# Row products, block sums and the order of the attention rounds in a chain of two small transformer blocks

## The chip, the cores and the metric

The kernel runs on one core of a Trainium2 chip. The metric is the device time of one execution in microseconds; the kernel before has a median of 1409.66 us in 3 runs (1409.54 to 1411.51). Everything is computed in float32.

## What is computed

Input x has 256 tokens of width 1024. It passes two blocks of two layers each.

Block 1, per layer: `mod = silu(c) @ w_ada + b_ada` is cut into shift, scale and gate; `u = rms_norm(x, g) * (1 + scale) + shift`; `z = u @ w_in` is cut into queries, keys, values and gates of three attentions (A: 8 heads over the 64 best keys of an indexer; B: window with sinks, 8 query heads and 2 key heads; C: stick-breaking, 8 heads) and three merge gates. Each attention's output times `silu(gate)` goes through its own matrix, the three are added under `sigmoid(m)`, and `x + gate * (merged @ w_out)` is the next x. A last `rms_norm` ends the block.

Block 2 has the 256 tokens of x and 256 context tokens. Per layer: `mod` as above, from a condition for x and one for the context (so two columns); `h = x * (1 + scale) + shift`; four mixers of 256 columns each: H (a gated linear scan in both directions), G (grouped attention), F (differential attention), N (window attention with sinks); queries of x see the keys of x and of the context. Then `x_new = layer_norm(alpha * x + gate * (y @ w_out))`. In layer 0 the context gets the same treatment; in layer 1 it only gives keys, values and the scan's final states. The kernel reads 222.6 MB from HBM, nearly all of it weights, each once.

## The kernel before

**Layout.** Activations lie transposed: channels on the 128 partitions, tokens (256) in the free dimension, 8 blocks of channels. Weights come in units of 1 MB (128 x 2048 numbers) through a ring of five slots; SP's queue starts the transfer of unit n + 5 when unit n has been used (`stream`). A unit of a projection is 16 matmuls of 128x128 by 256 columns, which the profile shows as 32 records. Results go to one of three PSUM banks ("events"), in turn; an item waits until the bank that it takes has been drained (`drained`) and signals when it is full (`full`).

**Order.** The whole program is one list of items per section (`prologue`, `one0`, `one1`, `two0`, `two1`). Every engine walks the same list and does its own part of each item, in order; semaphores count the parts. `one0` and `one1` are block 1's layers, and `one1` also has the context's attentions of block 2 at its end; `two0` and `two1` are block 2's layers. There is no planner: the lists are written by hand, and `weave`, `behind`, `lay` and `lay_scan` put items between one another.

**Attention.** A section has a list of jobs (10, 18, 16, 16). A job has these steps: logits (TensorE, to a PSUM tensor that all jobs share), mask or maximum (VectorE), exponentials (ScalarE), scaling (VectorE, item "soft"), transposition ("turn": TensorE, then a copy to PT by ScalarE), value product ("mix": TensorE, then a copy to y by VectorE). For the stick-breaking jobs (C) turn is a product with triangular matrices, then clamp (VectorE), exponential (ScalarE) and select (GpSimd). `weave` makes rounds of them; for round n the list is: logits n, slot 2n-1 of `fill`, soft n, mix n-2, turn n-1, slot 2n. The slots hold projections, the picks of the 64 best keys, scan steps and the like. `("half", item)` does the first half of a unit's work, so that its halves can stand in two slots.

**Modulation.** `mod` for later layers is computed in two ways. "By rows" (`mvr` and `mvs`, the two halves of a unit): the unit holds 256 columns of the matrix as rows, and VectorE multiplies a 128x1024 half with silu(c) on all partitions and sums it, one instruction per condition (line 1751); `bias` adds b_ada. "By TensorE" (`mva`, line 965): silu(c) is the 128x32 weight in four strips, the result is copied out (line 1739), transposed (`ada`, line 979), added up over the strips (lines 1778 and 1781). In the kernel before, block 2's layer-1 groups 0 to 3 (shift and scale) go by TensorE in `two0`, groups 4 and 5 (gate) in `two1`.

**Norms.** Squares of the 8 blocks of channels are added over blocks and partitions by 8 matmuls with a matrix of ones (`stats` line 1001; `mean` and `var` line 1330). Squares of block 1's x come from ScalarE after each `out` (line 1494); mean and variance of block 2's layer norm are taken from x after each `out`/`outb` (evictions at lines 2072 and 2084).

**Scan.** The mixer H is computed in nine levels. `prep` makes the operands of a level (GpSimd gaps at lines 2282 to 2288, ScalarE exponential, VectorE products at lines 2153 and 2155), `level` is 8 matmuls into two banks (line 1257) and VectorE copies them under a mask (line 2172), `hout` is the last product.

## Time and profile before

| what | value |
|---|---|
| median of 3 runs | 1409.66 us |
| profiled execution, its own time | 1411.23 us |
| its span, first to last instruction | 1409.5 us |
| TensorE busy | 1367.1 us, 97% |
| weight loads busy | 1123.4 us, 80% |
| VectorE busy | 655.1 us, 46% |
| ScalarE busy | 419.7 us, 30% |
| GpSimd busy | 165.5 us, 12% |
| moved by DMA | 224.93 MB, 160 GB/s over the span |
| mean granted clock of TensorE | 0.995 of full |

PE is TensorE's matmuls, PEld its weight loads, DVE VectorE, ACT ScalarE, POOL GpSimd, SP the queue that starts transfers. L1022 is line 1022 of the kernel. x32 is a count of records. A matmul's end is modelled, so that the times from one group's start to the next one's say more than the lengths. A group of rows of one line shows the start, the length, the engine, the line, the tiles and, in brackets, the engine's idle time before it and what ended it.

### The profile page before, as it was taken

How to read it: one execution, taken by the hardware profiler on the slowest of the kernel's cores; microseconds unless marked ns; L12 is line 12 of the kernel's file. 1: busy time of each engine (PE TensorE's matmuls, PEld its weight loads, DVE VectorE, ACT ScalarE, POOL GpSimd, SP SyncE). 2: the span in 40 equal slices, each digit the busy share in tenths (PEclk: the TensorE clock that was granted, in tenths of full speed). 3: DMA queues.
4: the chain of work that ended last, by engine and by line, in shares of the span. 5: the costliest groups of instructions: out<-in, count | busy, mean ns of one | idle time of the engine just before them, and what ended most of it. 6: DMA issues, size and time to landing. Idle time of an engine off the chain costs nothing.

```text
span 1409.5 us, 19281 instructions
## 1 busy us (share of the span) xinstructions
PE 1367.1 (97%) x7590; PEld 1123.4 (80%) x7590; DVE 655.1 (46%) x1457; ACT 419.7 (30%) x773; POOL 165.5 (12%) x191
## 2 busy tenths in 40 slices
PE   6999999999999999999999999999999999999996
PEld 4888787888888888888888888877777788887764
DVE  1447776445223554424144421245683632566466
ACT  2322222411021222333323313332343512433442
POOL 0201200000020120001021100003230000242000
PEclk9999999999999999999999999999999999999998
DMA  9636555568534433444333433455332343422240
GB/s 385 245 110 255 193 213 210 222 262 310 187 121 149 179 120 120 180 162 145 126 118 124 145 120 116 142 190 187 123 111 90 102 152 121 182 103 90 90 150 31
DMA packets 31916, 224.93 MB, mean 160 GB/s; under 512 B 3921, under 2 KB 4049, under 8 KB 5073
## 3 DMA queue, kind: packets, MB, share of 16 engines
q1 hardware_dynamic: 31824, 223.68, 43.0%
q8 instruction: 61, 1.00, 0.3%
q14 instruction: 31, 0.25, 0.0%
HBM read 222.62 MB, written 1.05 MB: 159 GB/s over the span
## 4 chain that ended last, share of the span: by engine, by line
PE 88%; DVE 7%; issue 2%; ACT 1%; DMA 1%; POOL 1%; SPq 0%; DVEq 0%; ACTq 0%; POOLq 0%
PE event L1022 45%; PE event L1013 9%; PE event L1166 6%; PE event L1230 5%; PE logits L1098 4%; PE mixed_out L1154 3%; PE turns L1117 3%; PE event L1257 2%; PE event L1191 2%; PE event L1196 2%; PE logits L989 1%; PE event L965 1%; PE event L1330 1%; PE event L1001 1%; DVE logits L1850 1%
## 5 line engine op out<-in xcount | busy, mean ns | idle before, releaser
L1022 PE MATMUL event<-u,ring 128*128 128x256 f32 x3072 | 683.3, 381 | 9.0 <-DMA ring<-in_w 4.3
L1022 PEld LDWEIGHTS event<-u,ring 128*128 128x128 f32 x3072 | 576.9, 190 | 101.5 <-issue 18.2
L1013 PE MATMUL event<-ring,u 128*128 128x256 f32 (+1 forms) x704 | 151.1, 372 | 0.0
L1013 PEld LDWEIGHTS event<-ring,u 128*128 128x128 f32 x704 | 127.4, 190 | 21.4 <-issue 5.3
L2308 POOL TENSOR_TENSOR raw<-raw,tables 128x512 f32<-128x512 f32 (+1 forms) x28 | 44.6, 1593 | 701.9 <-DVE turned L1824 518.8
L1427 ACT ACTIVATE region<-event 128x512 f32<-128x512 f32 x72 | 43.0, 597 | 275.4 <-PE event L1022 275.1
L1463 ACT ACTIVATE S<-logits,stat 128x512 f32<-128x512 f32 (+2 forms) x160 | 83.9, 536 | 130.0 <-DVE stat L1865 120.6
L1230 PE MATMUL event<-region,ring 128*128 128x256 f32 x384 | 85.0, 380 | 0.0
L1166 PE MATMUL event<-region,ring 128*128 128x256 f32 x384 | 84.2, 380 | 0.0
L1230 PEld LDWEIGHTS event<-region,ring 128*128 128x128 f32 x384 | 72.3, 190 | 12.2 <-issue 2.7
L1166 PEld LDWEIGHTS event<-region,ring 128*128 128x128 f32 x384 | 72.7, 190 | 10.8 <-issue 1.0
L1479 ACT ACTIVATE PT<-turns 128x1024 f32<-128x1024 f32 (+1 forms) x52 | 44.7, 860 | 81.7 <-PE turns L1117 81.2
L1842 DVE TENSOR_REDUCE stat<-logits 128x2 f32<-128x1024 f32 (+1 forms) x32 | 39.2, 1224 | 53.2 <-PE logits L1098 52.7
L1098 PE MATMUL logits<-region 64*128 64x256 f32 (+4 forms) x320 | 59.9, 475 | 2.9 <-ACT S L1463 1.4
L1751 DVE CUSTOM_DVE_ANT_0 region<-ring,u 128x1024 f32<-128x1024 f32 x48 | 59.1, 1231 | 1.7
L2172 DVE COPY_PREDICATED region<-tables,event 128x512 f32<-128x512 uint32 x42 | 30.9, 735 | 58.5 <-PE event L1257 57.4
L1924 DVE COPY region<-mixed_out 128x256 f32<-128x256 f32 (+3 forms) x60 | 21.7, 362 | 75.3 <-PE mixed_out L1154 65.1
L1154 PE MATMUL mixed_out<-PT,region 128*64 128x128 f32 (+2 forms) x584 | 54.8, 296 | 0.8 <-ACT PT L1479 0.8
L1154 PEld LDWEIGHTS mixed_out<-PT,region 128*64 128x64 f32 x584 | 38.3, 136 | 16.5 <-issue 13.4
L1117 PE MATMUL turns<-consts,S 128*128 128x128 f32 x336 | 47.9, 281 | 0.0
L1751 DVE CUSTOM_DVE_ANT_0 region<-ring,region 128x1024 f32<-128x1024 f32 x32 | 40.4, 1263 | 11.2 <-issue 5.0
L2282 POOL TENSOR_TENSOR region<-region 128x256 f32<-128x256 f32 x24 | 16.0, 667 | 248.6 <-PE event L1257 156.5
(246 smaller groups left out, 1343.7 us busy)
## 6 DMA issues: line engine op xcount, KB each, us to landing
ring<-in_w SPq DMA_DIRECT2D x196, 1024.0 KB, 4.9
region<-in_quick SPq DMA_DIRECT2D x8, 1024.0 KB, 18.7
region<-in_rows SPq DMA_DIRECT2D x1, 1536.0 KB, 8.3
tables<-in_two SPq DMA_DIRECT2D x1, 1472.0 KB, 7.9
x<-in_x SPq DMA_DIRECT2D x1, 1024.0 KB, 7.2
u<-in_cond_rows SPq DMA_DIRECT2D x1, 1024.0 KB, 7.7
x<-in_ctx SPq DMA_DIRECT2D x1, 1024.0 KB, 7.1
out<-x SPq DMA_DIRECT2D x4, 256.0 KB, 2.2
```

The lines of the kernel that those rows point to most:

```text
L1013: ins = mm(bank[:, t * 256:t * 256 + width], mem.u[:, q, k, t * P:(t + 1) * P], wt[:, k * 256:k * 256 + width], start=k == 0, stop=k == KB ...
L1022: ins = mm(bank[:, j * 256:(j + 1) * 256], wt[:, k * 256 + j * P:k * 256 + j * P + P], mem.u[:, q, k, :], start=k == 0, stop=k == KB - 1)
L1098: ins = mm(out, q, k, start=True, stop=True)
L1117: ins = eng.transpose(mem.TR[:, i * P:(i + 1) * P], S[:, at:at + P], c["ident"])
L1154: ins = mm(out, value_of(mem, job, m, kt), turned[:, :, kt, :], start=kt == 0, stop=kt == tiles - 1)
L1166: ins = mm(bank[:, j * 256:(j + 1) * 256], wt[:, at:at + P], mem.one["y"][:, 4 * br + k, :], start=k == 0, stop=k == 3)
L1230: ins = mm(bank[:, j * 256:(j + 1) * 256], wt[:, at:at + P], src[:, k, :], start=k == 0, stop=k == KB - 1)
L1427: act(dst, split2(bank), func, scale=scale).then_inc(drained[e % BANKS], 1)
L1463: ins = act(S[:, m * K:(m + 1) * K], mem.LG[:, m * K:(m + 1) * K], ACT.Exp, bias=stat[:, 1, m:m + 1], accum_out=stat[:, 2, m:m + 1])
L1479: act(mem.PT[:, n % 2, 0:cols], mem.TR[:, 0:cols], ACT.Copy).then_inc(sems["turns_copied"], 1)
L1751: ins = eng.tensor_tensor_reduce(out=mem.scratch, in0=part, in1=times, scale=1.0, scalar=0.0, op0=ALU.mult, op1=ALU.add, accum_out=mem.mod ...
L2308: tt(shape(mem.raw), shape(mem.raw), wide(cosine, width // T), ALU.mult).then_inc(mine, 1)
```

## The change

It does the following:

- In `weave` the order of round n becomes: logits n, the scan levels of slot 2n-1, mix n-2, then `hout` and the rest of slot 2n-1, soft n, turn n-1, slot 2n. Levels in slots behind a turn stay where they were.
- `lay_scan` puts the latent scans' steps in every second slot, which is one that follows logits, so one step a round; before, a step came every 1.4 (`two0`) or 1.34 slots (`two1`).
- Block 2's layer-1 groups 0 to 3 (8 units) are computed by rows: two units at the end of `one0`'s list of them, six in `one1`. The units of `mva` and the `ada` steps of `two0` are gone.
- A unit by rows with two conditions stands whole (four instructions) behind a job's turn; before, its halves stood behind logits and turn. Units with one condition stand whole behind the logits of jobs that are not C. Behind the merges and projections at the end of `one0` the halves stay single.
- In `one1` the first feed of the context (`mod`, `feed`) moves from logits 4 to logits 7, the context's first projections come after five of the six gate projections, and the load of block 2's tables on SP's queue moves from the last gate unit to the context's `kk` unit and also waits for the picks.
- Blocks 0 to 5 of the squares (both `stats` of block 1) and of x (both `mean`) are added on VectorE ahead of the evictions of the third and fourth `out` (`sum_pair`), and TensorE makes 3 matmuls with ones in place of 8. The squares of the context's variance are added down to two blocks (`sum_squares`), and TensorE makes 2 in place of 8. The variance of x keeps its 8.

```diff
 LEVELS = [0, 1, 2, 4, 8, 16, 32, 64, 128]
+SUMMED = (0, KB - 2, KB - 1)
 A_Q, A_K, A_V, A_G, I_Q, I_K, I_W = 0, 512, 1024, 1536, 2048, 2304, 2368
...
     return layer_of(sec, q) if name in CARRIED else 0 if q else sec.layer
+def beside(items, kinds):
+    return [i for i in items if i[0] in kinds]
 def weave(jobs, fill):
...
     def more():
-        if fill:
-            s.extend(fill.pop(0))
+        return fill.pop(0) if fill else []
     for n in range(jobs + 2):
+        items = []
         if n < jobs:
+            items = more()
             s.append(("logits", n))
-            more()
-            s.append(("soft", n))
+            s += beside(items, ("level",))
         if n >= 2:
             s.append(("mix", n - 2))
+        s += beside(items, ("hout",)) + [i for i in items if i[0] not in ("level", "hout")]
+        if n < jobs:
+            s.append(("soft", n))
         if 1 <= n <= jobs:
             s.append(("turn", n - 1))
-            more()
+            s += more()
     return s
 def group(tag, g):
...
     s += [("merge", 2, 0), ("merge", 2, 1)] + [("out", i, (0,)) for i in range(4)]
-    spots = [(kind, n) for n in range(len(JOBS_ONE)) for kind in ("logits", "turn")]
-    spots += [proj("m", 0, i) for i in range(5, 12)] + [("merge", br, half) for br in range(3) for half in (0, 1)][:-1]
-    spots.sort(key=s.index)
-    both = halves_of_rows(units_of("v0", 0, 1, 2, 3, 4, 5))
-    for spot, half in zip(spots, both):
+    both = halves_of_rows(units_of("v0", 0, 1, 2, 3, 4, 5) + units_of("v1", 0))
+    one = halves_of_rows(units_of("w1", 0, 1, 2, 3) + units_of("w0", 4, 5))
+    for n, job in enumerate(JOBS_ONE):
+        behind(s, ("turn", n), both.pop(0) + both.pop(0))
+        if job.kind != "C":
+            behind(s, ("logits", n), one.pop(0) + one.pop(0))
+    tail = [proj("m", 0, i) for i in (5, 6, 7)] + [("merge", 0, 0), ("merge", 0, 1)] + [proj("m", 0, i) for i in (8, 9, 10)]
+    for spot, half in zip(tail, both):
         behind(s, spot, half)
-    one = halves_of_rows(units_of("w1", 0, 1, 2, 3) + units_of("w0", 4, 5))
-    for k, spot in enumerate([("turn", n) for n, job in enumerate(JOBS_ONE) if job.kind == "C"] + spots[len(both):]):
-        behind(s, spot, one[2 * k] + one[2 * k + 1])
-    assert k == len(one) // 2 - 1
+    for spot in (tail[-1], proj("m", 0, 11), proj("m", 0, 11), ("merge", 1, 0), ("merge", 1, 1), ("merge", 2, 0)):
+        at = s.index(spot) + 1
+        while s[at][0] in ("mvr", "mvs", "bias"):
+            at += 1
+        s[at:at] = one.pop(0) + one.pop(0)
+    assert len(tail) == len(both) and not one
     picks_beside(s)
...
     out += [([("level", 0, LEVELS[i - 1])] if i else []) + [("prep", 0, m)] for i, m in enumerate(LEVELS[1:])]
-    return out + [[("level", 0, LEVELS[-2]), ("prep", 0, "qc")], [("level", 0, LEVELS[-1])], [], [("hout", 0)], [("sq", "h0")],
+    return out + [[("level", 0, LEVELS[-2]), ("prep", 0, "qc")], [("level", 0, LEVELS[-1])], [("hout", 0)], [("sq", "h0")],
                   [("norm", "h0")]]
...
     fill[8].append(("small",))
-    fill += [[proj("kk", 1)], [proj("vv", 1)], [proj("gq", 1), ("sq", "gk1")], [proj("gate", 0, 0), ("norm", "gk1")],
-             [proj("gate", 0, 1), ("sq", "gq1")], [proj("gate", 0, 2), ("norm", "gq1")], [proj("gate", 0, 3)],
-             [proj("gate", 0, 4)], [proj("gate", 0, 5)], [proj("hq", 1)], [proj("ff", 1)], [proj("fb", 1)],
+    fill += [[proj("gate", 0, i)] for i in range(5)]
+    fill += [[proj("kk", 1)], [proj("vv", 1)], [proj("gq", 1), ("sq", "gk1")], [proj("hq", 1), ("norm", "gk1"), ("sq", "gq1")],
+             [proj("ff", 1), ("norm", "gq1")], [proj("gate", 0, 5)], [proj("fb", 1)],
              [proj("hi", 1), proj("nq", 1)], [("gates",), proj("m", 0, 0), ("gap", 1), ("decay", 1), proj("m", 0, 1)]]
...
     s += weave(len(jobs), fill) + [i for f in fill for i in f]
-    behind(s, ("logits", 4), [("mod", "v0"), ("feed", 1, "v0")])
-    rows = halves_of_rows(units_of("w1", 4, 5))
-    for k, n in enumerate((1, 2, 7, 8)):
-        behind(s, ("logits", n), [i for half in rows[2 * k:2 * k + 2] for i in half])
+    behind(s, ("logits", 7), [("mod", "v0"), ("feed", 1, "v0")])
+    both, one = halves_of_rows(units_of("v1", 1, 2, 3)), halves_of_rows(units_of("w1", 4, 5))
+    for n in range(len(both) // 2):
+        behind(s, ("turn", n), both[2 * n] + both[2 * n + 1])
+    for k, n in enumerate((1, 2, 8, 9)):
+        behind(s, ("logits", n), one[2 * k] + one[2 * k + 1])
     picks_beside(s)
...
             slot[0:0] = piece
-def lay_scan(fill, start, step, steps):
+def lay_scan(fill, start, steps):
     for n, items in enumerate(steps):
-        fill[start + int(n * step)] += items
+        fill[max(start + 2 * (n - 2), 0) if n < 12 else start + n + 6] += items
 def script_two0():
...
     fill[0] += [proj("hq")]
-    lay_scan(fill, 3, 1.4, latent_scan())
+    lay_scan(fill, 3, latent_scan())
     fill[24] += [("silu", 0), ("gate", 0, 0)]
...
         fill[h] += items
-    groups = list(enumerate((1, 3, 5, 7)))
-    for g, h in groups:
-        fill[h] += group("v1", g)
-    lay(fill, 1, 24, [proj("nq"), out(1), ("rot", "nq", 0), out(2), out(3), ("mean", 1), proj("fk"), ("var", 1),
-                      proj("fq"), ("rot", "fk", 0), ("mod", "v1"), proj("fv"), ("rot", "fq", 0), proj("hi"), ("feed", 1, "v1"), proj("ff", 1),
+    lay(fill, 1, 24, [proj("nq"), out(1), ("rot", "nq", 0), out(2), out(3), proj("fk"), ("mean", 1),
+                      proj("fq"), ("var", 1), ("rot", "fk", 0), ("mod", "v1"), proj("fv"), ("rot", "fq", 0), proj("hi"), ("feed", 1, "v1"), proj("ff", 1),
                       proj("fb", 1), proj("g"), proj("g", 0, 1), proj("g", 0, 2), proj("g", 0, 3)])
     lay(fill, 25, 32, [proj("hi", 1)] + [("outa", i, (0,)) for i in range(3)])
-    for g, h in groups:
-        fill[h + 1].append(("ada", g, "v1"))
     s += weave(len(jobs), fill)
...
     fill = [[] for _ in range(2 * len(jobs))]
-    lay_scan(fill, 1, 1.34, latent_scan())
+    lay_scan(fill, 1, latent_scan())
     fill[15] += [("silu", 0)]
     fill[20] += [("gate", 0, 0)]
-    lay(fill, 0, 20, [proj("nq"), proj("g"), ("rot", "nq", 0), proj("g", 0, 1), proj("fk", 1), proj("fk"), proj("g", 0, 2), ("rot", "fk", 0),
+    lay(fill, 0, 19, [proj("nq"), proj("g"), ("rot", "nq", 0), proj("g", 0, 1), proj("fk", 1), proj("fk"), proj("g", 0, 2), ("rot", "fk", 0),
                       proj("fq"), proj("g", 0, 3), ("rot", "fq", 0), proj("hi"), proj("fv"), proj("fv", 1)])
...
                 eng.dma_start(mem.par2[:, :, :], dram["par2"]).then_inc(sems["rest_in"], 16)
-            if sec.name == "one1" and item == ("proj", "gate", 5, (0,)):
+            if sec.name == "one1" and item == ("proj", "kk", 0, (1,)):
                 eng.wait_ge(sems["rope_done"], w.at("rope_done", 8))
+                eng.wait_ge(sems["picked"], w.at("picked", 2))
                 eng.wait_ge(sems["maxed"], w.at("maxed", 3))
...
                     eng.wait_ge(drained[e % BANKS], w.fills(e - BANKS))
+                    eng.wait_ge(sems["squares_summed"], w.at("squares_summed", 1))
                 bank = mem.bank[e % BANKS]
-                for k in range(KB):
-                    if k % 2 == 0:
+                for k in range(KB) if sec.name == "prologue" else SUMMED:
+                    if k % 2 == 0 and (k or sec.name == "prologue"):
                         eng.wait_ge(sems["squares_ready"], w.at("squares_ready", k // 2 + 1))
...
                 q = item[1]
-                src = mem.x if kind == "mean" else mem.u
                 eng.wait_ge(drained[e % BANKS], w.fills(e - BANKS))
                 bank = mem.bank[e % BANKS]
-                for k in range(KB):
-                    if k % 2 == 0 and kind == "mean":
-                        ev = w.first[("outb", (q,))] + k // 2 if q == 0 else w.first[("out", k // 2, (q,))]
-                        eng.wait_ge(drained[ev % BANKS], w.fills(ev))
-                    elif k % 2 == 0:
-                        eng.wait_ge(sems["vsquares"], w.at("vsquares", 4 * sec.index(("mean", q)) + k // 2 + 1))
-                    ins = mm(bank[:, 0:T], c["ones"], src[:, q, k, :], start=k == 0, stop=k == KB - 1)
+                if kind == "mean":
+                    eng.wait_ge(sems["x_summed"], w.at("x_summed", sec.index(item) + 1))
+                    mm(bank[:, 0:T], c["ones"], mem.u[:, q, 0, :], start=True, stop=False)
+                    ev = w.first[("outb", (q,))] + 3 if q == 0 else w.first[("out", 3, (q,))]
+                    eng.wait_ge(drained[ev % BANKS], w.fills(ev))
+                    for k in SUMMED[1:]:
+                        ins = mm(bank[:, 0:T], c["ones"], mem.x[:, q, k, :], start=False, stop=k == KB - 1)
+                elif q == 1:
+                    eng.wait_ge(sems["vsquares_summed"], w.at("vsquares_summed", 1))
+                    for k in range(2):
+                        ins = mm(bank[:, 0:T], c["ones"], mem.u[:, q, k, :], start=k == 0, stop=k == 1)
+                else:
+                    for k in range(KB):
+                        if k % 2 == 0:
+                            eng.wait_ge(sems["vsquares"], w.at("vsquares", 4 * sec.index(("mean", q)) + k // 2 + 1))
+                        ins = mm(bank[:, 0:T], c["ones"], mem.u[:, q, k, :], start=k == 0, stop=k == KB - 1)
                 ins.then_inc(full[e % BANKS], 1)
...
     Walk(eng).run(body)
+def sum_pair(eng, sems, w, to, src, i, links, done):
+    two = slice(2 * i - 2, 2 * i)
+    eng.tensor_tensor(to[:, 0:2, :], src[:, 0:2, :] if i == 2 else to[:, 0:2, :], src[:, two, :], ALU.add).then_inc(sems[links], 1)
+    eng.wait_ge(sems[links], w.linked())
+    if i == 3:
+        eng.tensor_tensor(to[:, 0, :], to[:, 0, :], to[:, 1, :], ALU.add).then_inc(sems[done[0]], 1)
+        eng.wait_ge(sems[done[0]], w.at(*done))
+def sum_squares(eng, sems, w, u, n, links):
+    for i in range(4):
+        eng.wait_ge(sems["vsquares"], w.at("vsquares", n + i + 1))
+    eng.tensor_tensor(u[:, 0:4, :], u[:, 0:4, :], u[:, 4:8, :], ALU.add).then_inc(sems[links], 1)
+    eng.wait_ge(sems[links], w.linked())
+    eng.tensor_tensor(u[:, 0:2, :], u[:, 0:2, :], u[:, 2:4, :], ALU.add).then_inc(sems["vsquares_summed"], 1)
+    eng.wait_ge(sems["vsquares_summed"], w.at("vsquares_summed", 1))
 def scalar(eng, sems, mem, dram):
...
                 for n in range(4):
+                    if n >= 2:
+                        sum_pair(eng, sems, w, mem.u[:, q], mem.x[:, q], n, "dve_links", ("x_summed", 2))
                     eng.wait_ge(full[(e + n) % BANKS], w.fills(e + n))
...
                 mod = mem.mods[f"w{sec.name[-1]}" if one else "v0" if q else f"v{sec.layer}"]
+                if kind == "out" and i >= 2 and one:
+                    eng.wait_ge(sems["squares_ready"], w.at("squares_ready", i))
+                    sum_pair(eng, sems, w, mem.u[:, 0], mem.u[:, 0], i, "dve_links", ("squares_summed", 1))
+                elif kind == "out" and i >= 2:
+                    sum_pair(eng, sems, w, mem.u[:, q], mem.x[:, q], i, "dve_links", ("x_summed", 1))
                 eng.wait_ge(full[e % BANKS], w.fills(e))
...
                 eng.wait_ge(sems["centred"], w.at("centred", 4 * n))
+            elif kind == "var" and item[1] == 1:
+                sum_squares(eng, sems, w, mem.u[:, 1], 4 * sec.index(("mean", 1)), "dve_links")
             elif kind == "affine":
...
...
```

## Rows read from the trace of the kernel before

**Rows 1.** Page: busy us (share of the span), instructions

```profile
PE 1367.1 (97%) x7590; PEld 1123.4 (80%) x7590; DVE 655.1 (46%) x1457; ACT 419.7 (30%) x773; POOL 165.5 (12%) x191
```

**Rows 2.** Busy times by stretch: stretch, its us, engines' busy us, clock, DMA

```profile
72.00:395.00 323.00, 315.68 (x1586) 268.11 (x1586) 177.86 (x394) 75.13 (x141) 19.26 (x17) 1.00 0.56 212
395.00:853.00 458.00, 456.00 (x2478) 383.73 (x2477) 174.70 (x445) 128.66 (x255) 53.83 (x58) 1.00 0.39 142
853.00:1185.00 332.00, 325.82 (x1891) 263.75 (x1891) 156.33 (x321) 111.20 (x194) 41.71 (x48) 0.99 0.37 132
```

**Rows 3.** Waits of TensorE from 72 us on: total us, times, longest

```profile
PE event L1022 <- DMA ring<-in_w: 4.3, 2, 2.5
...
PE event L1257 <- DVE x L2084: 2.1, 1, 2.1
PE event L1022 <- DVE region L2172: 1.7, 1, 1.7
...
PE event L965 <- DVE mod_raw L1778: 1.0, 1, 1.0
```

**Rows 4.** Timeline of TensorE, products with the modulation matrix: start us, us

```profile
937.51 1.93 PE L965 MATMUL event<-ring,cond 128*32 128x256 f32 x32
...
963.23 0.60 PE L979 MATMUL event<-consts,strips 128*128 128x128 f32 x4
963.76 1.13 PE L1098 MATMUL logits<-region 64*128 64x512 f32 x4
...
971.73 3.58 PE L965 MATMUL event<-ring,cond 128*32 128x256 f32 x32
975.25 3.72 PE L1230 MATMUL event<-region,ring 128*128 128x256 f32 x16
```

**Rows 5.** Stretch of the third of these groups: PE busy, clock, DMA

```profile
972.00:976.00 4.00, 4.00 (x36) 0.61 0.17 72
```

**Rows 6.** Timeline, ends of the first layer and of the first latent layer

```profile
383.41 3.62 PE L1001 MATMUL event<-u,consts 128*128 128x256 f32 x16
...
384.65 0.63 ACT L1494 ACTIVATE u<-x 128x512 f32<-128x512 f32 x1 [6.28 <-DVE x L2084]
...
1164.15 3.62 PE L1330 MATMUL event<-x,consts 128*128 128x256 f32 x16
...
1164.42 0.88 DVE L2072 SCALAR_TENSOR_TENSOR x<-event,mod_v,x 128x256 f32<-128x256 f32 x2 [0.85 <-PE event L1213]
1167.60 3.62 PE L1022 MATMUL event<-u,ring 128*128 128x256 f32 x16
```

**Rows 7.** Timeline of TensorE, a round of the first layer

```profile
112.13 1.14 PE L1098 MATMUL logits<-region 64*128 64x256 f32 x8
113.19 7.17 PE L1022 MATMUL event<-u,ring 128*128 128x256 f32 x32
120.30 1.08 PE L1154 MATMUL mixed_out<-PT,region 128*64 128x512 f32 x4
121.31 1.09 PE L1117 MATMUL turns<-consts,S 128*128 128x128 f32 x8
122.24 7.07 PE L1022 MATMUL event<-u,ring 128*128 128x256 f32 x32
129.24 0.70 PE L1060 MATMUL logits<-region 64*128 64x256 f32 x4
```

**Rows 8.** Timeline of TensorE, a level in front of a value product

```profile
1305.57 1.16 PE L1257 MATMUL event<-region 64*128 64x128 f32 x16
1306.66 1.09 PE L1154 MATMUL mixed_out<-PT,region 128*64 128x128 f32 x16
```

**Rows 9.** VectorE: L1751, ns min/median/max; L2189, busy us, mean ns

```profile
L1751 DVE CUSTOM_DVE_ANT_0 region<-ring,region x32: 1224/1225/1530, 158.9 to 581.9; 128x1024 f32<-128x1024 f32 x32
...
L2189 DVE TENSOR_TENSOR x<-x,mean 128x512 f32<-128x512 f32 x8 | 5.0, 684 | 0.1
```

**Rows 10.** Stretch with the most work on VectorE, columns as rows 2

```profile
1010.00:1043.00 33.00, 33.00 (x222) 25.99 (x221) 29.30 (x66) 9.92 (x19) 16.18 (x19) 1.00 0.20 67
```

15 lines of the change are left out of this document (4 added, 11 removed).

## The prediction, made before the result was known

> **What bounds the kernel now.** I read the page's busy times first. The reader is to see that TensorE is busy for 97% of the span, its weight loads for 80% and VectorE for 46% [rows 1]. A share of busy time is an average, so the stretches come next. The program has five: start, first layer (72 to 395 us), second layer with the context's jobs (395 to 853), first latent layer (853 to 1185), last latent layer. In the three that the change touches most TensorE is busy for 315.7 of 323, 456.0 of 458 and 325.8 of 332 us, VectorE for 178, 175 and 156 [rows 2]. So the time is TensorE's instructions plus few gaps, and a change pays by what it takes off that engine, or loses by the waits it adds. The list of what TensorE waited for shows how few gaps there are: 4.3 us for two transfers of the ring (both before 215 us), and 2.1, 1.7 and 1.0 us for VectorE, all three in the first latent layer [rows 3].
>
> **A. Products with the layer-1 modulation matrix, groups 0 to 3, leave TensorE.** Each group is two units and one transposition step. A group's 32 records take 1.9 us (start 937.51), but the one at 971.73 takes 3.5 us, to the next start at 975.25; the transpositions take 0.53 us, from 963.23 to 963.76 [rows 4]. The long one is the same work at half speed: the granted clock was 0.61 over 972 to 976 us, the lower of its two levels (1.2 and 2.4 GHz) for most of it, and what went before was the 2.1 us wait [rows 3, 5]. Removed: 3 x 1.9 + 3.5 + 4 x 0.53 = 11.3 us. In exchange VectorE makes 8 units x 2 halves x 2 conditions = 32 row products more, 1.23 us each (1.53 at worst) [rows 9], 39 us; 8 of them in the first layer, 24 (29.5 us) in the second. Per job they stand as a block of four, 5 us, behind the job's turn. What they delay is what is queued behind them on VectorE: the copy of a value projection, then the next job's mask or maximum, for which TensorE waits a projection later. A projection takes 7 us on TensorE [rows 7], so the block lies beside it. In the second layer VectorE has 283 us free [rows 2]: cost 0. If that cover is gone, a block costs up to 5 us. I take 0; the ends are 0 and 30 us. The ring gets six units more in the second layer and eight fewer in the first latent one; TensorE met no late transfer after 215 us, so 0. In SP's queue the load of block 2's tables moves from the last gate unit to the context's first projection and also waits for the last pick; behind it stand the ring's transfers, which have five slots' lead, and the pick stands two jobs ahead of it: 0.
>
> **B. Sums of squares and of x.** A product with the matrix of ones is 2 of the 16 records that take 3.45 us [rows 6], so 0.43 us. Five of eight go from both statistics of block 1 and from both means, six of eight from the variance of the context.
> - Second layer's statistics, mean of the context, its variance: these stand amid projections, and the sums are ready a projection earlier: 2 x 2.15 + 2.6 = 6.9 us.
> - First layer's statistics: TensorE now runs without a gap from 383.41 for 3.62 us. The last square starts at 384.65 and takes 0.63 us, so that blocks 6 and 7 cannot start before 385.3, and 0.86 us later it is 386.2 instead of 387.0 [rows 6]: 0.8 us, not 2.15.
> - Last mean: the last eviction starts at 1164.42 and takes 0.88 us [rows 6]. In front of it VectorE now adds 0.69 us of 512 columns [rows 9] and about half of that for 256, of which only some 0.85 us was idle; the eviction ends near 1165.7, the mean near 1166.7 instead of 1167.8: 1.1 us.
>
> B = 8.8 us. Were every sum in the way of an eviction that TensorE awaits, B would be 0.
>
> **C. The order.** Before, a job's round is logits, projection, value product, turns, projection. The logits use 64 rows of the array and the value product 64 columns, the rest the whole. A projection that follows logits and precedes a value product takes 7.11 us from start to start, one that follows turns 7.00; 16 records of one in an unbroken stream take 3.45 us [rows 6], 32 so 6.91; turns behind a value product take 0.93 us (0.86 of it work) and the value product 1.01 [rows 7]. In the new round logits, value product, projection, turns, projection, there is one switch of tile shape fewer. It saves 0.11 on the projection and 0.07 on the turns; the value product behind row tiles starts 1.09 us after the level before it [rows 8], no dearer than the 1.06 us from logits to a projection [rows 7]. I take 0.16 us a round; 8 + 16 + 14 + 14 = 52 rounds have both steps: 8.3 us. A scan level now goes behind the logits too; of 27 levels 4 stay (behind turns, second layer), some ten stood there already, and 13 lose a switch of their own at 0.2 us: 2.6 us. C = 10.9 us, bounds 0 and 16 (0.2 us for each of about 80 switches).
>
> The Trainium skill (TensorEngine Tiling (Array Packing), Key Properties) says that changing the tiling mode drains TensorE. The trace agrees, at 0.1 to 0.2 us a switch [rows 7, 8]. By that rule alone, with the value product to projection switch kept dear, C would be the 8.3 us or less.
>
> The value product is also issued a projection earlier (7 us, or 3.6 us in the latent layers). It waits for the copy of the turns of two jobs ago, behind which at least half a projection still stands; for a stick-breaking job it waits for clamp, exponential and select, which the logits in front of it wait for already. Price 0, at worst 0.5 us a round.
>
> **D. Waits that go.** In the first layer a unit's two halves no longer lie on both sides of the next logits, with picks between, so its ring slot comes free half a round sooner: 4.3 us [rows 3]. In the first latent layer the scan's steps come once per round instead of once per 0.7 round, the group for which TensorE waited 1.0 us is gone, and with it the events that made a level or a projection ask for a bank not yet drained: 2.1 + 1.7 + 1.0 = 4.8 us [rows 3]. D = 9.1 us.
>
> **Given back.** Shorter rounds meet the same VectorE work. From 1010 to 1043 us it is busy for 29.3 of 33 us [rows 10]. Those rounds lose some 2.5 of 13.5 us on TensorE, while the scan's work on VectorE thins by a third per round. I put back 6.6 us, somewhat more than the 4.8 us of waits that stand there today; bounds 0 and 20.
>
> **Sum.** 11.3 + 8.8 + 10.9 + 9.1 - 6.6 = 33.5 us. The profiled execution took 1411.23 us, of which 1409.5 is its span and 1.7 lies around it; the median of the runs is 1409.66. Against that median: 1376.2 us, forecast 1376 (1377.7 by the profiled execution's own time). The forecast's own spread is 1368 to 1384.
>
> **Rivals.**
> - R1, VectorE becomes the bound of the first latent layer. For it: 29.3 of 33 us [rows 10]. Against it: 156 of 332 over the whole stretch [rows 2]. Then A's 11.3 us and the 4.8 us of D turn into other waits, and with what I give back already: about 1390. Chance 0.14.
> - R2, the order buys nothing: the switch from value product to projection costs what the others save. C falls away: 1387. Chance 0.12.
> - R3, TensorE's stream has slack in itself, so removed records do not pay in full. For it: weight loads are busy for only 80% [rows 1]. Against it: 32 records in a row keep 6.91 us everywhere, and a weight load is nearly the length of what it hides behind. A and B would pay 80%, 16 instead of 20 us, and C likewise: 1382. Chance 0.05. The Trainium skill (Perfetto Trace Analysis, Identifying the Most-Contended Engine) says that matmul busy time does not tell how close one is to the roofline and that weight loads' share does; by it a fifth of TensorE would be free.
> - R4, the sums don't shorten anything: TensorE waits for VectorE's additions in all five places. B is gone: 1385. Chance 0.05.
> - R5, slower. The blocks of row products keep VectorE from clamp and mask in time, and TensorE waits for the next logits: the six blocks of the second layer and two in the first cost 5 us each, 41 us, against 33.5: 1417. It decides only from 4 us a block upward, where today's projection hides 7. Chance 0.03.
>
> The forecast keeps 0.61.
>
> **Numbers.** The range is 1364 (no giving back, C at its upper bound) to 1392 (R1); R5 and a sum of two rivals stay outside. What a measurement can tell from no change is about 0.2%, 2.8 us. Faster by more 0.96, within it 0.01, slower 0.03.
>
> **What would show it.** TensorE's busy time falls by some 31 us (A without waits, 26 products of B, most of C); VectorE's rises by about 43 (39 of products, some 9 of sums, 4 of copies and additions less). The groups of 128x32 weights keep 64 of 192 records in the latent layers. The first latent layer is about 20 us shorter, the first layer 6, the second 5, the last 2. A round of the second layer takes 16.95 instead of 17.11 us. No wait for the ring before 215 us. The forecast is wrong if TensorE's waits for VectorE in the first latent layer sum to over 15 us (R1), if projection and value product rows keep their sum (R2), or if TensorE waits for masks, maxima or clamps in the second layer (R5).

## The result, and the profile after

The changed kernel takes 1391.13 us (median of 4 runs, 1388.96 to 1392.24) against 1410.59 us for the kernel before on the same chip (4 runs, 1409.54 to 1412.46). The ratio is 0.9859, 95% interval 0.984 to 0.9877: 19.5 us faster. The forecast was 1376 us, 33.5 us faster. The time lies inside the range given and 7 us outside the forecast's own spread. Median and interval belong to the timed runs. The profile below is of the fastest of the four (1388.96 us), 22.3 us shorter than the profiled execution of the kernel before.

The page of the changed kernel first, busy times with their share of the span, to be read against [rows 1]:

```profile
PE 1339.2 (97%) x7394; PEld 1114.7 (80%) x7394; DVE 704.8 (51%) x1525; ACT 423.5 (31%) x776; POOL 168.2 (12%) x191
```

TensorE does 27.9 us less (31 forecast), VectorE 49.7 us more (43 forecast). So the work left TensorE nearly as planned. Its busy time fell by 27.9 us and the span by 22.3, so its gaps grew by 5.6 us, where the forecast had them shrink. The list of TensorE's waits from 60 us on (total us, times, longest) shows them:

```profile
PE logits L1100 <- DVE region L2134: 6.1, 1, 6.1
PE event L1335 <- DVE u L1363: 2.5, 1, 2.5
PE event L1024 <- ACT u L1397: 2.4, 1, 2.4
PE event L1232 <- DVE x L2121: 2.3, 2, 2.1
PE event L1176 <- DVE strips L1769: 2.1, 1, 2.1
...
PE event L1241 <- ACT rs L1531: 1.0, 1, 1.0
```

The ring waits of [rows 3] are gone. The third of these lines was there before, with the same 2.4 us. New are the 6.1 us, the 2.5 us, and 2.1 us of the last latent layer, where the kernel before waited 0.7 us. Two waits of 1.0 us for ScalarE in the first latent layer are new too: the one of line 1241 above, and one of a value product for its copy of the turns (line 1156). Every kernel here with the new order has both, and the one with the old order has neither. The wait of 2.1 us for an eviction (line 2121, before line 2084 or 2072) is no longer for a level as in [rows 3], but for output units.

To find the layer of each, I cut every trace into five stretches at the same four places of TensorE's work: behind the first group of the indexer's dots, and behind the statistics (or variance) that end each of the first three layers. In this table, worked out from the starts in the timelines, a column is the length of a stretch in the profiled execution; the second column is the median of the timed runs.

```
kernel          median    start   first  second  latent 1  latent 2
before         1410.59    61.59  327.79  473.81    311.32    234.99
after          1391.13    59.02  321.03  478.15    295.47    233.53
mva_back       1397.58    60.08  321.02  478.46    302.47    233.57
no_sums        1397.00    62.26  321.59  480.76    296.04    235.25
old_order      1399.98    59.77  322.41  480.94    299.90    234.78
norm_early     1390.80    59.02  321.03  477.38    297.13    233.54
feed_early     1383.81    59.10  321.03  470.41    293.83    233.53
sum_behind     1391.20    59.39  321.02  479.06    293.10    236.73
row_late       1390.15    60.61  321.03  478.40    295.48    232.98
best           1380.27    61.77  321.03  471.61    291.83    233.06
feed_turn      1381.04    61.63  321.01  471.59    293.81    233.56
best_turn      1380.15    60.35  321.02  470.39    291.82    233.02
ctx_old        1391.66    58.97  321.01  470.26    302.47    233.59
split_halves   1411.33    60.20  341.54  479.70    295.47    233.59
```

Two things about reading it. The start, which no kernel here changes, is between 58.97 and 62.26 us long; 2.6 of the 22.3 us between the two profiled executions are of that kind. And where the work of a stretch is the same, its length repeats to 0.1 us (321.01 to 321.03 in ten kernels), unless the clock falls in it. In the latent layers a fall makes a stretch 1.6 us longer, or twice that. In the second layer kernels with the same work differ by up to 1.5 us (478.15, 478.40, 479.06, 479.70; 470.41 and 471.61; 471.59 and 470.39), so smaller differences there say nothing. More on the clock stands at the end.

The changed kernel's layers against the kernel before: first -6.8 (-6 forecast), second **+4.3** (-5 forecast), first latent -15.9 (-20), last -1.5 (-2). The error is in the second layer, and a smaller one in the first latent layer.

**Second layer.** The changed kernel's timeline around the long wait (start us, us, engine, line; in brackets idle time before, and what ended it):

```profile
598.81 1.02 PE L1241 MATMUL event<-rs,consts 128*128 128x512 f32 x2
...
599.06 1.28 ACT L1457 ACT_TABLE_LOAD   x1 [1.71 <-PE event L1024]
600.35 0.60 ACT L1457 ACTIVATE region<-event 128x512 f32<-128x512 f32 x1
600.97 1.28 ACT L1536 ACT_TABLE_LOAD   x1
602.26 0.69 ACT L1536 ACTIVATE rs<-event,eps 128x512 f32<-128x512 f32 x1
602.97 1.28 ACT L1538 ACT_TABLE_LOAD   x1
604.26 0.63 ACT L1538 ACTIVATE rs<-rs 128x512 f32<-128x512 f32 x1
605.00 0.75 DVE L2134 SCALAR_TENSOR_TENSOR region<-region,small,rs 128x512 f32<-128x512 f32 x1 [8.04 <-ACT rs L1538]
605.90 2.08 PE L1100 MATMUL logits<-region 64*128 64x256 f32 x8 [6.07 <-DVE region L2134]
607.91 1.87 PE L1156 MATMUL mixed_out<-PT,region 128*64 128x128 f32 x16
```

The logits of job 10 read the context's query, whose norm product ends at 599.8. Between the two stand three table loads of 1.28 us, the eviction of the forget projection, logarithm and exponential, and VectorE's scaling. VectorE was idle for 8.04 us before its scaling: it is named as releaser, but it was itself waiting for ScalarE. The Trainium skill (ScalarE: Activation LUTs, What ACT_TABLE_LOAD costs) puts a switch at about 2.66 us, about half of it the load and half a drain. Here each load is 1.28 us as there, but the next instruction starts at its end, 3.8 us for the three; no run here shows the drain. The logits then take 2.08 us and the value product 1.87, both nearly twice the usual ([rows 7] has 1.14 for the same logits, [rows 8] 1.09 for such a value product). The stretches behind the two waits of the second layer (stretch, its us, engines' busy us, clock, DMA share, GB/s), the last line from the kernel before, behind the same wait as the second:

```profile
605.90:610.00 4.10, 4.10 (x25) 3.10 (x26) 1.50 (x3) 0.37 (x1) 0.00 (x0) 0.56 0.00 0
380.05:386.00 5.95, 5.95 (x20) 4.66 (x21) 2.72 (x6) 3.44 (x7) 0.00 (x0) 0.71 0.00 0
389.38:395.38 6.00, 6.00 (x25) 4.09 (x26) 2.72 (x6) 3.45 (x7) 0.00 (x0) 1.00 0.00 0
```

A granted clock of 0.56 means 1.2 GHz for most of the 4.1 us; against 2.4 GHz throughout that costs 4.1 x 0.44 = 1.8 us. 0.71 over 5.95 us costs 5.95 x 0.29 = 1.7. In the kernel before that stretch had 1.00. So the second layer's sum is: 4.95 us gained (sums 2.15, order 2.8), 6.1 + 1.8 + 1.7 lost, +4.65, where 4.3 is measured.

**First latent layer.** Two of VectorE's sums stand where TensorE waits. Timeline of the changed kernel:

```profile
962.43 0.69 DVE L1350 TENSOR_TENSOR u<-x 128x512 f32<-128x512 f32 x1
963.15 0.88 DVE L2121 SCALAR_TENSOR_TENSOR x<-event,mod_v,x 128x256 f32<-128x256 f32 x2
...
964.18 5.38 PE L1232 MATMUL event<-region,ring 128*128 128x256 f32 x16 [2.09 <-DVE x L2121]
970.26 3.62 PE L1232 MATMUL event<-region,ring 128*128 128x256 f32 x16
...
997.47 1.23 DVE L1361 TENSOR_TENSOR u<-u 128x1024 f32<-128x1024 f32 x1
998.73 0.69 DVE L1363 TENSOR_TENSOR u<-u 128x512 f32<-128x512 f32 x1
...
999.57 0.67 PE L1335 MATMUL event<-u,consts 128*128 128x256 f32 x2 [2.48 <-DVE u L1363]
```

The sum for the mean (line 1350) delays by 0.7 us the eviction that frees a bank; the 16 records behind it take 5.38 us instead of 3.62, since the clock fell; of six kernels with this same wait it fell in four (last section), so that 1.65 us of this layer are partly chance. The sum of squares starts when TensorE already waits for it.

**The last mean** came as forecast, answering to [rows 6]:

```profile
1144.98 0.67 PE L1327 MATMUL event<-u,consts 128*128 128x256 f32 x2 [0.59 <-DVE u L1353]
1145.80 1.13 PE L1331 MATMUL event<-x,consts 128*128 128x256 f32 x4
1146.77 3.62 PE L1024 MATMUL event<-u,ring 128*128 128x256 f32 x16
```

From the end of the last output product (0.59 us before 1144.98) to the next projection it is 2.4 us, before 3.45: 1.0 us of the 1.1.

The second layer's statistics take 1.29 us to the next projection, 2.15 less than the 3.45 of [rows 6]:

```profile
856.91 1.46 PE L1003 MATMUL event<-u,consts 128*128 128x256 f32 x6
858.20 4.05 PE L1024 MATMUL event<-u,ring 128*128 128x256 f32 x18
```

### The profile page after: what moved, and what is told of

Read it like the earlier page. It is cut to its first block, busy times and chain, and to the rows that moved or that the text cites. A ratio compares the mean times of both kernels' runs of the same rounds, so it can differ in the third digit from the quotient of the medians.

```text
span 1387.2 us, 18957 instructions
## 1 busy us (share of the span) xinstructions
PE 1339.2 (97%) x7394; PEld 1114.7 (80%) x7394; DVE 704.8 (51%) x1525; ACT 423.5 (31%) x776; POOL 168.2 (12%) x191
## 4 chain that ended last, share of the span: by engine, by line
PE 87%; DVE 4%; issue 3%; DMA 2%; ACT 2%; SPq 1%; POOL 0%; DVEq 0%; ACTq 0%; POOLq 0%
PE event L1024 45%; PE event L1015 11%; PE event L1168 6%; PE event L1232 5%; PE logits L1100 4%; PE mixed_out L1156 3%; PE turns L1119 2%; DMA region<-in_quick 2%; PE event L1259 2%; PE event L1198 2%; PE event L1193 2%; PE turns L990 1%; PE logits L990 1%; PE turns L1114 1%; PE logits L1114 1%
## 5 line engine op out<-in xcount | busy, mean ns | idle before, releaser
L1781 DVE CUSTOM_DVE_ANT_0 region<-ring,u 128x1024 f32<-128x1024 f32 x80 | 103.8, 1298 | 2.8
L1872 DVE TENSOR_REDUCE stat<-logits 128x2 f32<-128x1024 f32 (+1 forms) x32 | 39.2, 1224 | 59.2 <-PE logits L1100 58.7
L1509 ACT ACTIVATE PT<-turns 128x1024 f32<-128x1024 f32 (+1 forms) x52 | 44.7, 860 | 55.2 <-PE turns L1119 54.5
L1156 PEld LDWEIGHTS mixed_out<-PT,region 128*64 128x64 f32 x584 | 39.0, 139 | 19.0 <-issue 11.1
L2190 DVE TENSOR_TENSOR region<-region 128x512 f32<-128x512 f32 x24 | 19.1, 797 | 57.8 <-ACT region L1549 31.2
L1880 DVE CUSTOM_DVE_ANT_0 logits<-logits,tables 128x128 f32<-128x128 f32 (+2 forms) x48 | 22.9, 477 | 50.1 <-PE logits L1100 45.6
L1100 PEld LDWEIGHTS logits<-region 64*128 64x128 f32 (+1 forms) x320 | 24.8, 188 | 28.4 <-issue 23.2
```

The source lines that it names most:

```text
L1100: ins = mm(out, q, k, start=True, stop=True)
L1156: ins = mm(out, value_of(mem, job, m, kt), turned[:, :, kt, :], start=kt == 0, stop=kt == tiles - 1)
L1509: act(mem.PT[:, n % 2, 0:cols], mem.TR[:, 0:cols], ACT.Copy).then_inc(sems["turns_copied"], 1)
L1781: ins = eng.tensor_tensor_reduce(out=mem.scratch, in0=part, in1=times, scale=1.0, scalar=0.0, op0=ALU.mult, op1=ALU.add, accum_out=mem.mod ...
L1872: eng.tensor_reduce(stat[:, 0, 0:nm], mem.LG[:, 0:nm * K].rearrange("p (m k) -> p m k", m=nm), AX.X, ALU.max).then_inc(mine, 1)
```

## The experiments

Four kernels share a chip and the runs of the kernel before in each set; those had medians of 1410.47, 1411.46 and 1410.77 us.

**1. Each part undone by itself.** `mva_back`: the groups go back to TensorE, and the row products for them leave the first two layers. The places of the context's input and projections stay as changed.

```diff
-    both = halves_of_rows(units_of("v0", 0, 1, 2, 3, 4, 5) + units_of("v1", 0))
+    both = halves_of_rows(units_of("v0", 0, 1, 2, 3, 4, 5))
...
+    groups = list(enumerate((2, 4, 6, 8)))
+    for g, h in groups:
+        fill[h] += group("v1", g)
...
+    for g, h in groups:
+        fill[h + 1].append(("ada", g, "v1"))
```

> The changed kernel with groups 0 to 3 of the layer-1 modulation products back on TensorE in the first latent layer, one group every other slot (2, 4, 6, 8), and VectorE's 32 row products for them gone; sums and order stay as changed. Theory (term A pays): four groups of 1.9 us and four transposition steps of 0.53 us at full clock come back, 9.7 us: 1400.8 us (1399 to 1403), the first latent layer about 305 instead of 295.5 us, the second layer unchanged. Rival (VectorE bounds the first latent layer, so TensorE's work there is partly free): 1392 to 1396 us. Rival below nothing (the added row products cost the first two layers more than A gave): 1391 us or less.

Measured 1397.58 us (1395.77 to 1398.61, 4 runs; ratio to the kernel before 0.9907, 0.9892 to 0.9922). In the table the first latent layer is 7.0 us longer. This lies between theory and first rival: the term pays, less the waits it brought. With the groups back TensorE waits 1.1 us for evictions twice (line 983 is the groups' transposition) instead of 2.3, and 1.1 instead of 2.5 for the sum of squares, and no half clock follows. Against an execution of the changed layer without a fall of the clock (293.81, `feed_turn`) it is 8.7 us. The second layer keeps its length (478.46 us) and its wait of 6.1 us, though VectorE makes none of the 24 added row products there. So VectorE's load is not what makes that wait:

```profile
PE logits L1103 <- DVE region L2137: 6.1, 1, 6.1
...
PE event L983 <- DVE x L2124: 1.1, 1, 1.1
PE event L1235 <- DVE x L2124: 1.1, 1, 1.1
PE event L1338 <- DVE u L1366: 1.1, 1, 1.1
```

`no_sums`: products with ones over all eight blocks again.

```diff
-                for k in range(KB) if sec.name == "prologue" else SUMMED:
+                for k in range(KB):
...
-                    sum_pair(...)
-                sum_squares(...)
```

> The changed kernel with all eight products with the matrix of ones back in the five places, and VectorE's sums gone. Theory (term B pays where no wait replaced it): 8.8 us as predicted less the 2.5 us for which the changed kernel waits for the sum of the context's squares: 6.3 us, 1397.4 us (1396 to 1399). Rival (the sums pay nothing, TensorE waits for them): 1391 us. Rival (the additions on VectorE also cost evictions): below 1391 us.

Measured 1397.00 us (1394.52 to 1397.61, 4 runs; ratio 0.9898, 0.988 to 0.9916), as the theory has it in the sum. The table says where: 0.6 us in the first layer, 2.6 in the second, only **0.6 in the first latent one**, where 5.85 had been forecast, and 1.7 in the last one, which has no such product; that 1.7 is the clock (below). The first latent layer of this kernel has no fall of the clock (its wait for the eviction is 1.4 us) and that of the changed kernel has one. Against the changed layer without it (293.82) the sums are worth 2.2 us there. By layers that is 3.7 us, or 5.4 at the same clock, and that the total of 5.9 met the 6.3 expected is partly luck.

`old_order`: `weave`, `lay_scan` and the latent scan's list of the kernel before.

```diff
             s.append(("logits", n))
-            s += beside(items, ("level",))
+            more()
+            s.append(("soft", n))
         if n >= 2:
             s.append(("mix", n - 2))
-        s += beside(items, ("hout",)) + [i for i in items if i[0] not in ("level", "hout")]
-        if n < jobs:
-            s.append(("soft", n))
         if 1 <= n <= jobs:
             s.append(("turn", n - 1))
-            s += more()
+            more()
```

> The changed kernel with the order of before in the weaving of jobs (logits, slot, value product, turns, slot), and the latent scans spread by 1.4 and 1.34 slots as before; row products and sums stay as changed. Theory (term C pays): 52 rounds at 0.16 us and 13 levels at 0.2 us come back, 10.9 us, and part of the 4.8 us of waits of the first latent layer: 1402 us (1400 to 1406); a round of the second layer takes 17.11 us. Rival (the order buys nothing once the waits it makes in the latent layers are counted): 1390 to 1394 us.

Measured 1399.98 us (1399.56 to 1401.01, 5 runs; ratio 0.9926, 0.9914 to 0.9938). That is the lower bound of the theory's interval, far from the rival's. By layers 1.4, 2.8, 4.4 and 1.25 us, 9.9 in all: the order pays. Not all of it is switches of the array. In the first latent layer the two waits for VectorE, 2.3 and 2.5 us in the changed kernel, are 3.7 us each here, and the clock falls behind both:

```profile
PE event L1331 <- DVE u L1359: 3.7, 1, 3.7
PE event L1228 <- DVE x L2117: 3.7, 1, 3.7
```

These are 2.6 us of waits and a second fall (1.65 us), against the 2.0 us of waits for ScalarE that the old order lacks; some 2 us of the 4.4 are left for the rounds (an estimate, 14 rounds at 0.15). A round of the second layer in the changed kernel and then in this one (start to start):

```profile
460.90 1.13 PE L1100 MATMUL logits<-region 64*128 64x256 f32 x8
461.96 1.08 PE L1156 MATMUL mixed_out<-PT,region 128*64 128x512 f32 x4
462.97 7.17 PE L1024 MATMUL event<-u,ring 128*128 128x256 f32 x32
469.98 1.04 PE L1119 MATMUL turns<-consts,S 128*128 128x128 f32 x8
470.86 7.07 PE L1024 MATMUL event<-u,ring 128*128 128x256 f32 x32
477.86 0.70 PE L1062 MATMUL logits<-region 64*128 64x256 f32 x4
```

```profile
462.85 1.13 PE L1096 MATMUL logits<-region 64*128 64x256 f32 x8
463.92 7.17 PE L1020 MATMUL event<-u,ring 128*128 128x256 f32 x32
471.02 1.08 PE L1152 MATMUL mixed_out<-PT,region 128*64 128x512 f32 x4
472.03 1.09 PE L1115 MATMUL turns<-consts,S 128*128 128x128 f32 x8
472.96 7.07 PE L1020 MATMUL event<-u,ring 128*128 128x256 f32 x32
479.96 0.70 PE L1058 MATMUL logits<-region 64*128 64x256 f32 x4
```

16.96 us against 17.11 (16.95 was forecast): the projection 7.01 instead of 7.10, the turns 0.88 instead of 0.93, and the value product no dearer behind logits (1.01).

**2. Why the second layer lost.** `norm_early` gives the context's query more room.

```diff
-    fill += [[proj("gate", 0, i)] for i in range(5)]
+    fill += [[proj("gate", 0, i)] for i in range(4)]
...
-             [proj("ff", 1), ("norm", "gq1")], [proj("gate", 0, 5)], [proj("fb", 1)],
+             [proj("gate", 0, 4), ("norm", "gq1")], [proj("ff", 1)], [proj("gate", 0, 5)], [proj("fb", 1)],
```

> The changed kernel with one thing moved: in the second layer the context's projections start one slot earlier (gate unit 4 goes behind them), so that the gate projection and then the forget projection stand between the normalisation of its query and the first logits that read it. Theory (the normalisation stands too near): the changed kernel's trace shows 6.1 us of waiting for VectorE's normalised query from 599.8 us on, behind three ScalarE table loads of 1.28 us, and then 2 us more for logits and a value product at half clock. Both go: 1391.1 - 8 = 1383 us (1381 to 1385), and the second layer is about 470 us instead of 478. Rival (the wait only moves): ScalarE's table loads then delay an exponential, and the next value product waits for it: 1388 to 1391 us.

Measured 1390.80 us (1389.88 to 1391.85, 4 runs; ratio 0.986, 0.9846 to 0.9874). The time falls into the rival's interval, by another mechanism than either: the wait for the query is gone, and another stands in its place, some 50 us earlier, the longest of TensorE in the second layer:

```profile
PE event L1024 <- DVE u L2007: 4.8, 1, 4.8
```

Line 2007 is the context's scaled input (`feed`), which the change had moved from logits 4 to logits 7. So it was moved to job 6 as well (`feed_early`); that place is too early for the result, since the row products of the last of the eight units then read the context's input in place of the conditions; the instructions are the same.

```diff
-    behind(s, ("logits", 7), [("mod", "v0"), ("feed", 1, "v0")])
+    behind(s, ("logits", 6), [("mod", "v0"), ("feed", 1, "v0")])
```

> As the kernel that starts the context's projections a slot earlier, and the context's normalised input too: its scale and shift go behind the logits of job 6 instead of job 7. Theory (the first of the two only traded one wait for another: its trace shows no wait for the query any more, but 4.8 us for VectorE's scaled input of the context before the first of these projections, and a granted clock of 0.91 around it): with both moved neither wait is there, 1391 - 8 = 1383 us (1381 to 1385), the second layer about 470 us. Rival (VectorE is so full of picks and row products there that the wait comes back in another place): 1388 to 1391 us.

Measured 1383.81 us (1379.68 to 1387.27, 4 runs; ratio 0.9804, 0.9783 to 0.9824), the second layer 470.41 us: theory. But why had it been put so late? The rows of the conditions lie in the buffer of the context's input (`self.cond_rows = self.u[:, 1]...`), and the added row products read them until the turn of job 5. `feed_turn` puts the feed right behind the last of them.

```diff
-    behind(s, ("logits", 7), [("mod", "v0"), ("feed", 1, "v0")])
...
+    behind(s, both[-1][-1], [("mod", "v0"), ("feed", 1, "v0")])
```

> As the kernel with the context's projections a slot earlier, but with the context's scaled input made right behind the last of VectorE's row products for the layer-1 vector (the turn of job 5) instead of behind the logits of job 7. The rows of the conditions that these products read lie where that input is written, so this is the earliest place that leaves both as they are. Theory: the wait for the query stays away and the one for the input too, one1 is about 470 us and the time 1383 us (1381 to 1386). Rival (the input is still late, the wait of 4.8 us returns): 1388 us or more.

Measured 1381.04 us (1379.71 to 1383.35, 4 runs; ratio 0.9791, 0.9777 to 0.9804), as the theory had it, the second layer 471.6 us. The longest wait of TensorE there is the one that was always there:

```profile
PE event L1024 <- ACT u L1397: 2.4, 1, 2.4
```

All 24 row products of this layer are still in place. So the loss is one of places: feed and query norm stood later than the row products require.

The other way round, `ctx_old` takes the row products out and with them the constraint, and puts the groups back on TensorE. The load of block 2's tables goes back to the last gate unit.

```diff
+    fill += [[proj("kk", 1)], [proj("vv", 1)], [proj("gq", 1), ("sq", "gk1")], [proj("gate", 0, 0), ("norm", "gk1")],
+             [proj("gate", 0, 1), ("sq", "gq1")], [proj("gate", 0, 2), ("norm", "gq1")], [proj("gate", 0, 3)],
...
-    behind(s, ("logits", 7), [("mod", "v0"), ("feed", 1, "v0")])
...
+    behind(s, ("logits", 4), [("mod", "v0"), ("feed", 1, "v0")])
```

> The changed kernel with groups 0 to 3 of the layer-1 products back on TensorE, and with what these allow: the context's scaled input behind the logits of job 4, its projections at their places of before, the normalisation of its query three slots ahead of the logits that read it. Sums and order stay as changed. Theory (the loss in the second layer belongs to the row products, since they hold the rows of the conditions where the context's input has to go): the second layer takes 469 to 470 us instead of 478, the first latent layer 302.5 as with the groups alone put back: 1397.6 - 9 = 1388.6 us (1387 to 1391), so that the row products as placed bring nothing or cost up to 2 us. Rival (the place of the context's projections has its loss from the new order, not from the rows): the second layer stays at 476 us or more, 1395 us or more.

Measured 1391.66 us (1387.99 to 1392.66, 4 runs; ratio 0.986, 0.9846 to 0.9873): 0.7 us above the interval of the theory, with its layers: 470.26 and 302.47 us. It is as fast as the changed kernel, whose ratio is 0.9859. So the row products with the places that the change gave the context brought nothing. With the repaired places (`feed_turn`) they bring 10.6 us against `ctx_old` by the medians, and 7.3 by the layers: 8.7 in the first latent one less 1.3 in the second, most of which is the clock (`best_turn`, with the same second layer as `feed_turn`, has 470.39).

**3. The smaller waits.** `sum_behind` moves the two sums for the context's mean behind the evictions.

```diff
-                elif kind == "out" and i >= 2:
-                    sum_pair(...)
                 eng.wait_ge(full[e % BANKS], w.fills(e))
...
+                if kind == "out" and i >= 2 and not one:
+                    sum_pair(...)
```

> The changed kernel with one thing moved: in the first latent layer VectorE's two sums for the mean of the context stand behind the evictions of output units 2 and 3 instead of in front of them. Theory: in the changed kernel's trace the sum of 0.69 us stands in front of an eviction for which TensorE waits 2.1 us, and 16 records of the next product then run at half clock, 1.8 us more; with every product of ones back that wait is 1.4 us and no half clock follows. So 0.7 + 1.8 = 2.5 us less: 1388.6 us (1387 to 1390), 0.7 us less if the half clock comes all the same. Rival (TensorE then waits for the sum before the mean): no change, 1391 us.

Measured 1391.20 us (1387.84 to 1393.43, 4 runs; ratio 0.9855, 0.984 to 0.987), no change in the median, so the rival's number. The trace has the theory's mechanism: the wait is 1.4 us, no half clock follows, and the first latent layer is 2.4 us shorter. Only 0.7 of that is clear of chance, since `feed_early` and `feed_turn` have no fall there either with the longer wait. The last layer, whose work is the same, took 3.2 us more in this execution: after its wait of 2.1 us the clock fell to 1.2 GHz. With four runs spread over 5.6 us the 2.4 us can't be seen in the time.

`row_late`: the row steps of the last layer one slot later.

```diff
-        fill[h + 1].append(("row", g))
+        fill[h + 2].append(("row", g))
```

> The changed kernel with the two row steps of the last latent layer (groups 4 and 5 of the layer-1 modulation) one slot later. Theory: the changed order puts one of them so close behind its products that TensorE waits 2.1 us for VectorE's copy, 0.7 us in the kernel before; in some executions the half clock follows (1.7 us more, as in the trace of the kernel with all products of ones). With the step a slot later 1.4 to 3 us are gone: 1388.5 us (1387.5 to 1390). Rival (the step is waited for by the shift and scale by rows that use it, at the end, so what it loses there comes back): 1391 us or more.

Measured 1390.15 us (1388.83 to 1391.38, 5 runs; ratio 0.9849, 0.9835 to 0.9862). The last layer is 0.55 us shorter; the wait of 2.1 us is gone and logits there wait 1.2 us for exponentials instead. Less than the theory's 1.4 us, and not the rival's loss; in time it is not told from zero.

**4. All together.** `best` has the repairs of 2 (with the feed of `feed_early`, so that here too the last unit reads the wrong input) and 3, and VectorE's sum of squares as an item of its own, ahead of its product:

```diff
-                      proj("fq"), ("var", 1), ("rot", "fk", 0), ("mod", "v1"), proj("fv"),
+                      proj("fq"), ("sum", 1), ("rot", "fk", 0), ("mod", "v1"), proj("fv"), ("var", 1),
```

> All of these together (context's projections and input a slot earlier, sums behind the evictions, row steps a slot later), and the sum of the context's squares on VectorE two half projections ahead of its product on TensorE, for which the changed kernel waits 2.5 us. Theory: 8 + 2.5 + 1.4 to 3 + 2.5 = 14.5 to 16 us less: 1376 us (1374 to 1379). Rival (each wait removed shows another behind it): 1383 us or more.

Measured 1380.27 us (1378.96 to 1380.98, 4 runs; ratio 0.9779, 0.9765 to 0.9792), above the theory's interval and below the rival's. With the feed where the rows allow it (`best_turn`):

> The same, with the two sums of the context's mean behind the evictions, the sum of its squares half a layer's round ahead of its product, and the two row steps a slot later: all repairs together. Theory: second layer 470 to 471.6 us, first latent layer 291.8, last one 233: 1380 us (1378 to 1382). Rival (the waits come back in the second layer): 1386 us or more.

Measured 1380.15 us (1377.17 to 1380.67, 5 runs; ratio 0.9779, 0.9766 to 0.9792): 30.6 us below the kernel before and 11 us below the changed one. The forecast for `best` took 2.5 us for the sum of squares; its wait only fell from 2.5 to 1.4 us, now for a ScalarE copy.

**5. Ring waits.** `split_halves` puts the first layer's row products on both sides of the logits again and, since there are two more units, doubles up the rest near the end.

```diff
+    spots = [(kind, n) for n in range(len(JOBS_ONE)) for kind in ("logits", "turn")]
...
+    for spot, half in zip(spots, both):
+        behind(s, spot, half)
```

> The changed kernel with the row products of the first layer placed as before: one half behind each logits and each turn, so that a unit's two halves lie on both sides of the next job's logits, and the rest doubled up behind the later ones. Theory (the ring slot is held longer, and TensorE meets late transfers again): 4 to 5 us of waits for the ring before 215 us, the first layer 325.3 instead of 321.0 us, 1395.5 us (1394 to 1397). Rival (the new order alone had removed these waits): no wait for the ring, 1391 us.

Measured 1411.33 us (1409.0 to 1413.99, 11 runs; ratio 1.0004, 0.9995 to 1.0013). Waits of TensorE before 215 us, then from 215 to 402:

```profile
PE event L1020 <- DMA ring<-in_w: 3.9, 1, 3.9
```

```profile
PE event L1164 <- DMA ring<-in_w: 9.1, 1, 9.1
...
PE event L1020 <- DMA ring<-in_w: 2.0, 1, 2.0
```

The theory's wait before 215 us is there, 3.9 us, so the new order alone had not removed it. The other 11.1 us of waits, and the lower clock around the long one (0.83 over 340 to 360 us, 0.91 over 360 to 380), come with the pile at the end, which neither theory had: a clean undoing of this step it is not, but it shows what the placement of row products can cost: 20.5 us in the first layer.

## Why the prediction was right in sign and 14 us off in size

- **C, 10.9 us: the price of a round was right, the total near.** The round is 16.96 us, 0.15 shorter. Undoing the order costs 9.9 us by layers and 8.9 by the medians, but that holds longer waits and a fall of the clock as well. The 2.6 us for the scan's levels were not tried by themselves. The earlier value product, priced at 0, waits 1.0 us once for its copy. R2 is wrong. The Trainium skill (TensorEngine Tiling (Array Packing), Key Properties) has the drain at a change of tiling mode; here a round with one change fewer is 0.15 us shorter.
- **D, ring waits, 4.3 us: right.** None are left, the first layer gained 6.8 us (undoing the order and the sums gives back only 1.4 and 0.6 of them), and 3.9 us come back with split units. The 4.8 us of the first latent layer did not all go: 2.1 us stand there for an eviction again, and 2.0 us for ScalarE are new.
- **A, 11.3 us: the products were sized nearly right, the cost of what replaced them was not.** The groups are worth 8.7 us in their layer at the same clock (7.0 in the profiled execution), not 9.7 to 11.3. Without them TensorE waits 4.8 us for evictions and the sum of squares instead of 3.3; that is part of what "given back" had put at 6.6 us. The step that failed is the second layer's **"cost 0"**. The prediction asked only whether VectorE had time for 24 more row products there. It had. The move of the context's feed and projections, which is part of the change, has no term in the sum. The row products read the rows of the conditions, which share the context's buffer, so the feed may not stand ahead of the last of them, at the turn of job 5. The change put it behind logits 7, the projections behind that, and the query's norm right in front of its first reader. That is 6.1 us and the low clock behind it. `mva_back` keeps this wait without a single added row product in the layer, and `feed_turn` is rid of it with all of them: 10.1 us less by the medians, 6.6 by the layer. So the sharing explains why the feed moved, and the places chosen are what cost the time.
- **B, 8.8 us: wrong in one place.** Stats of both layers 3.2 us by layers (2.95 forecast), the last mean 1.0 (1.1). The context's mean and variance, 4.75 us forecast, gave 1.2 us (2.2 at the same clock, less 1.0 for the last mean), and nothing where the clock fell as in the profiled execution. "The sums are ready a projection earlier" does not hold in a layer where VectorE is behind. R4, confined to this layer, is most of what happened there.
- **Given back, 6.6 us:** the right idea in the right layer, and too small by about what B lost there. R1 itself is wrong, though its 1390 us (1392 by its own terms) is the number nearest to the result: the waits for VectorE in the first latent layer sum to 5.4 us (2.5 + 2.3 + 0.6), not to over 15. The range ended at 1392 only because of R1, so that the result lies inside it by luck, and not for the reason that set its end.
- R3 is not needed: removed records paid in full wherever no wait stood behind them. The second layer's statistics take 1.29 us with 6 records and 3.45 with 16, 0.215 us a record both times. "32 records in a row keep 6.91 us everywhere" does not follow from the rows: a projection between other shapes takes 7.00 to 7.11 us in [rows 7]. By the rule of the Trainium skill (Perfetto Trace Analysis, Identifying the Most-Contended Engine) a fifth should have been free at 80% of weight loads; no run here shows that. R5 did not occur; no mask or maximum was late in the second layer.

The sum by layers without the start: 6.8 - 4.3 + 15.9 + 1.5 = 19.7 us, against 33 forecast. 9.3 of the missing 13.3 us are the second layer, 4.1 the first latent one.

## What to carry to other kernels

When work moves to an idle engine, follow its operands as well as its time: the buffer that it goes on reading keeps someone else's write waiting, and the loss appears several items later on another engine. Find the earliest place that the operands allow, and not just a safe one. Room between a producer and its reader is worth most where an engine has to change tables several times in between. And sums that spare TensorE a product pay only if they stand ahead of it by more than the queue of the engine that makes them.
